# First-tile turns ahead of the second's at three projections, gated sums on VectorE, the last store in halves, compressed turns between pieces

## The reference, cut to what matters

```python
def first_block(x, p, ...):
    ...                                                            # pooled and causal attention, out projection
    x = x + rms_norm(conv_ffn(h, w_up, conv_w, conv_b, w_down), g_ffn_post)
    x = x + (p @ w_ple) * sigmoid(x @ w_ple_gate)                  # "ple" and "pg" in the kernel
    return x

def second_block(x, mem, positions, ...):
    for i in range(2):
        proj = x @ (nsa_w_in if i == 0 else mla_w_in)              # "n" and "m" in the kernel
        mix = nsa_mixer(...) if i == 0 else mla_mixer(...)         # i == 0: keys and values are also compressed
        xa = memory_cross_attention(...)
        x = layer_norm(ALPHA * x + concat(mix, xa) @ w_out[i], ...)
        x = layer_norm(ALPHA * x + hier_moe(x, ...), ...)          # 16 experts, top 2 of one group
    return x

def compress(t, pe, w1, w2):                                       # for the compressed keys and values
    blk = t[:, tok_idx] + pe                                       # 15 windows of 32 tokens
    return silu(blk @ w1) @ w2
```

## Time and profile before

| | us |
|---|---|
| median of three runs | 1104.91 (1103.94 to 1108.32) |
| the profiled execution, its own time | 1108.64 |
| its span in the profile | 1106.5 |
| TensorE busy | 1047.6 (95% of the span) |
| VectorE busy | 478.0 (43%) |
| ScalarE busy | 380.6 (34%) |
| GpSimd busy | 110.5 (10%) |

### The profile page before, as it was taken

How to read it: one execution, slowest core, us unless ns; L and a number is a source line. 1 busy time by engine, 2 the same in 40 slices (tenths; PEclk the granted TensorE clock), 3 DMA queues, 4 the chain that set the end, 5 groups by cost and what they waited for, 6 DMA issues and landing times.

```text
span 1106.5 us, 15554 instructions
## 1 busy us (share of the span) xinstructions
PE 1047.6 (95%) x6071; PEld 720.3 (65%) x6071; DVE 478.0 (43%) x1019; ACT 380.6 (34%) x739; POOL 110.5 (10%) x147
## 2 busy tenths in 40 slices
PE   6999999999999999899999999989989999999983
PEld 6967899999878879668553434338657734344431
DVE  4644656666447644765411101217664411111214
ACT  4454445555335454763211101113472311011100
POOL 0621101111000100340000000000141000000000
PEclk9999999999999999999999999999999899999997
DMA  9853576555346426317899999993427699999992
GB/s 334 194 182 117 186 226 210 170 181 201 127 178 227 138 78 232 131 53 309 339 422 422 420 421 420 419 399 131 186 108 304 249 423 421 421 420 422 418 410 85
DMA packets 95070, 296.93 MB, mean 268 GB/s; under 512 B 11102, under 2 KB 44046, under 8 KB 71438
## 3 DMA queue, kind: packets, MB, share of 16 engines
q1 hardware_dynamic: 93406, 290.09, 68.4%
q0 software_dynamic: 1584, 5.77, 1.3%
HBM read 294.60 MB, written 1.25 MB: 267 GB/s over the span
## 4 chain that ended last, share of the span: by engine, by line
PE 79%; DMA 8%; DVE 6%; ACT 3%; issue 2%; POOL 0%; POOLq 0%; SPq 0%; DVEq 0%; ACTq 0%
PE ps L902 34%; PE ps L1276 17%; PE ps L1306 8%; DMA w<-in_moe_w_up 5%; PE ps L843 3%; PE ps L1255 3%; DMA spare<-in_moe_w_down 3%; PE ps L1317 2%; PE ps L973 2%; PE ps L1006 2%; PE ps L987 2%; PE ps L896 1%; PE ps L850 1%; PE ps L1131 1%; PE ps L1209 1%
## 5 line engine op out<-in xcount | busy, mean ns | idle before, releaser
L1517 DVE TENSOR_TENSOR plo<-w,phi 128x1024 fp32r<-128x1024 f32 (+3 forms) x143 | 175.4, 1242 | 158.0 <-ACT phi L2201 157.0
L2201 ACT CAST phi<-w 128x1024 fp32r<-128x1024 f32 (+3 forms) x143 | 144.5, 1028 | 169.8 <-PE ps L902 155.6
L1276 PE MATMUL ps<-w,arena 128*64 128x512 f32 x568 | 153.5, 595 | 3.9 <-DMA w<-in_moe_w_up 3.9
L902 PE MATMUL ps<-hTr,phi 128*128 128x256 f32 x472 | 134.1, 284 | 0.0
L902 PE MATMUL ps<-hTr,plo 128*128 128x256 f32 x472 | 133.6, 283 | 0.0
L902 PE MATMUL ps<-yTr,phi 128*128 128x256 f32 x472 | 133.5, 283 | 0.0
L1276 PEld LDWEIGHTS ps<-w,arena 128*64 128x64 f32 x568 | 47.8, 137 | 78.1 <-issue 77.3
L2020 DVE CAST hots<-ps 128x256 fp32r<-128x256 f32 x16 | 6.8, 425 | 207.2 <-PE ps L1288 179.7
L902 PE MATMUL ps<-phi,yTr 128*128 128x512 f32 (+2 forms) x240 | 92.5, 385 | 3.5 <-issue 1.9
L902 PE MATMUL ps<-phi,hTr 128*128 128x512 f32 (+2 forms) x240 | 93.2, 388 | 1.1 <-DVE yTr L1507 1.1
L902 PEld LDWEIGHTS ps<-hTr,phi 128*128 128x128 f32 x472 | 90.6, 192 | 0.2 <-issue 0.2
(11 more groups left out here) (313 smaller groups left out, 1725.4 us busy)
## 6 DMA issues: line engine op xcount, KB each, us to landing
w<-in_moe_w_gate SPq DMA_DIRECT2D x36, 1024.0 KB, 15.7
w<-in_moe_w_up SPq DMA_DIRECT2D x35, 1024.0 KB, 20.2
w<-in_moe_w_down SPq DMA_DIRECT2D x29, 1024.0 KB, 21.3
w<-in_w_up SPq DMA_DIRECT2D x22, 1024.0 KB, 7.3
arena<-in_moe_w_gate SPq DMA_DIRECT2D x19, 1024.0 KB, 17.7
arena<-in_moe_w_up SPq DMA_DIRECT2D x16, 1024.0 KB, 13.9
arena<-in_moe_w_down SPq DMA_DIRECT2D x15, 1024.0 KB, 12.9
w<-in_w_out SPq DMA_DIRECT2D x6, 2048.0 KB, 9.4
```

The source lines that it names most:

```text
L902: ins_ = e.matmul(o, l[a], r[b], start=first and i == 0, stop=last and i == 2, skip_group_check=group)
L1276: ins_ = e.matmul(bank[64 * ee:64 * ee + 64, :], xg[:, k, o:o + 64], half_view(i, kind, p, ee, ab)[:, c, :], start=(k == 0), stop=(k == 7))
L1517: e.tensor_tensor(plo[:, 0:m], slots[u % 3][:, j * m:j * m + m], phi[:, 0:m].bitcast(F32), ALU.subtract).then_inc(s_cut)
L2201: e.copy(pieces[p % 4][0][:, 0:m], slots[u % 3][:, j * m:j * m + m]).then_inc(s_cast)
```

## The change

Bank plan: "x2" is parted. Tile 0 is turned into banks 4 and 5 ahead of the "ple" blocks, tile 1 into two banks of the common turn ahead of the last "ple" block. All three projections may start tile 0's half of the first piece when tile 0's low halves are there. GpSimd cuts the first piece of m0 after its join.

```diff
         B.plan("dn", 4, [4, 5, 6, 7], own=False)
+        B.plan("x2a", 2, [4, 5])
         B.work("ple", 4)
-        B.work("x2", 4)
+        B.work("x2b", 2)
...
-            for t in range(2):
-                e.wait_ge(s_x[t], 7)
-                e.dma_start(out[0, t * 128:t * 128 + 128, :], x[:, t, :]).then_inc(s_out, 16)
-            e.wait_ge(s_out, 32)
+            e.wait_ge(s_x[0], 7)
+            e.dma_start(out[0, 0:128, :], x[:, 0, :]).then_inc(s_out, 16)
+            for hf in range(2):
+                e.wait_ge(s_x[1], 7 + hf)
+                e.dma_start(out[0, 128:256, hf * 512:hf * 512 + 512], x[:, 1, hf * 512:hf * 512 + 512]).then_inc(s_out, 16)
+            e.wait_ge(s_out, 48)
...
             def tok3_steps(bks, pair, n, p0, steps, each=2, rows=None):
                 for j in steps:
                     pc = cut(p0 + j)
                     for t in range(2):
+                        if rows and j == 0:
+                            for stage, i in rows[t]:
+                                e.wait_ge(*B.empty(stage, i))
...
+            e.wait_ge(s_x[0], 2)
+            turn_row("x2a", 0, 0, x)
             e.wait_ge(*loaded("ple"))
             await_empty("p")
             for o in range(4):
                 t, hf = o // 2, o % 2
+                if o == 3:
+                    e.wait_ge(s_x[1], 2)
+                    turn_row("x2b", 0, 1, x)
                 bk = claim("ple", o)
...
-            for t in range(2):
-                e.wait_ge(s_x[t], 2)
-                turn_row("x2", 2 * t, t, x)
-            keep_on(psum[4], 9)
-            await_empty("x2")
-            out_proj("pg", h1, first_piece("pg0"))
+            out_proj("pg", h1, first_piece("pg0"), [[(stage, 0), (stage, 1)] for stage in ("x2a", "x2b")])
...
                 turn_row("x3", 2 * t, t, x)
-                keep_on(psum[4], (4, 6)[t])
-            await_empty("x3")
-            tok3("n", 0, h1, 512, first_piece("n1"))
+                if t == 0:
+                    keep_on(psum[4], 4)
+            tok3("n", 0, h1, 512, first_piece("n1"), row_tiles("x3"))
...
             bks, p0 = two_banks("n", 6), first_piece("n4")
-            tok3_steps(bks, h1, 420, p0, range(3))
+            for j in range(2):
+                for i in range(3 * j, 3 * j + 2):
+                    turn_compressed(i)
+                tok3_steps(bks, h1, 420, p0, range(j, j + 1))
+                turn_compressed(3 * j + 2)
+            e.wait_ge(s_rope, 2)
+            turn_cols("ks", pjA, 1280 - 64, 5, 64)
+            tok3_steps(bks, h1, 420, p0, range(2, 3))
...
                 turn_row("x4", 2 * t, t, x)
-                keep_on(psum[4], (2, 5)[t])
-            await_empty("x4")
-            tok3("m", 0, h1, 416, first_piece("m0"))
+                if t == 0:
+                    keep_on(psum[4], 3)
+            tok3("m", 0, h1, 416, first_piece("m0"), row_tiles("x4"))
... VectorE
-            cut(p0, p0 + 2)
-            for t in range(2):
-                turned_low("x2", 2 * t, t, (hTr, yTr))
-            cut(p0 + 2, p0 + 4)
+            turned_low("x2a", 0, 0, (hTr, yTr))
+            cut(p0, p0 + 1)
+            turned_low("x2b", 0, 1, (hTr, yTr))
+            cut(p0 + 1, p0 + 4)
...
                 ins_ = e.tensor_tensor(sgm[:, t, half], sgm[:, t, half], pl[:, t, half], ALU.mult)
-                if t == 0:
-                    ins_.then_inc(s_gm)
-                else:
-                    own.step(ins_)
-                    settle()
-                    ins_ = e.tensor_tensor(x[:, t, half], x[:, t, half], sgm[:, t, half], ALU.add)
+                own.step(ins_)
+                settle()
+                ins_ = e.tensor_tensor(x[:, t, half], x[:, t, half], sgm[:, t, half], ALU.add)
...
                 if hf:
-                    cut(p0 + 8, p0 + 10)
+                    cut(p0 + 8, p0 + 9)
                 gated(1, hf)
...
             p0 = first_piece("m0")
-            cut(p0, p0 + 1)
             for t in range(2):
                 turned_low("x4", 2 * t, t, (hTr, yTr))
+            e.wait_ge(s_cut, p0 + 1)
             cut(p0 + 1, p0 + 4)
... ScalarE
-            cast(p0, p0 + 2)
+            turned_high("x2a", 0, 0, hTr)
+            cast(p0, p0 + 1)
             for o in range(4):
+                if o == 1:
+                    cast(p0 + 1, p0 + 2)
+                if o == 3:
+                    turned_high("x2b", 0, 1, hTr)
                 evac("ple", o, pl[:, t, hf * 512:hf * 512 + 512], B.ap("ple", o)[:, :])
-            for t in range(2):
-                turned_high("x2", 2 * t, t, hTr)
... GpSimd
-            for hf in range(2):
-                half = slice(hf * 512, hf * 512 + 512)
-                e.wait_ge(s_gm, hf + 1)
-                e.drain()
-                ins_ = e.tensor_tensor(x[:, 0, half], x[:, 0, half], sgm[:, 0, half], ALU.add)
-            ins_.then_inc(s_x[0])
...
             experts(0)
+            p0 = first_piece("m0")
+            phi, plo = (a[:, 0:piece[p0][2]] for a in pieces[p0 % 4])
+            e.wait_ge(s_cast, p0 + 1)
+            e.drain()
+            e.tensor_tensor(plo, slot_of("m0")[:, 0:piece[p0][2]], phi.bitcast(F32), ALU.subtract).then_inc(s_cut)
```

More of the change, by code:

```diff
@@ L907, in cut, with tok3_steps @@
                 return [a[:, 0:piece[p][2]] for a in pieces[p % 4]]
-            def tok3_steps(bks, pair, n, p0, steps, each=2):
+            def tok3_steps(bks, pair, n, p0, steps, each=2, rows=None):
                 for j in steps:
@@ L920, in two_banks, with tok3, row_tiles @@
                 return [claim(stage, i0 + t) for t in range(2)]
-            def tok3(stage, i0, pair, n, p0):
-                tok3_steps(two_banks(stage, i0), pair, n, p0, range(4))
+            def tok3(stage, i0, pair, n, p0, rows=None):
+                tok3_steps(two_banks(stage, i0), pair, n, p0, range(4), rows=rows)
+            def row_tiles(stage):
+                return [[(stage, 2 * t + c) for c in range(2)] for t in range(2)]
             def feat3(stage, i0, pair, n, chunk, p0):
@@ L939, in pairs, with out_proj @@
                 return (2 * c + h) * 128
-            def out_proj(stage, pair, p0):
-                tok3(stage, 0, pair, 512, p0)
+            def out_proj(stage, pair, p0, rows=None):
+                tok3(stage, 0, pair, 512, p0, rows)
                 bks = [claim(stage, 2 + t) for t in range(2)]
@@ L1113, in tensor_program, with turn_compressed @@
                 e.wait_ge(*B.empty("n", i))
[L1114 to L1123, removed]
-            e.wait_ge(s_rope, 2)
-            turn_cols("ks", pjA, 1280 - 64, 5, 64)
+            def turn_compressed(i):
+                kv, c = i // 3, i % 3 * 2
+                bk = claim("kc", i)
+                m = min(2, 5 - c)
+                for q in range(2 * m):
+                    c0 = 704 + kv * 256 + (c + q // 2) * 64
+                    w = 64 if c == 4 else 128
+                    ins_ = e.transpose(bk[0:w, q * 128:q * 128 + 128], pjA[:, q % 2, c0:c0 + w], ident)
+                ins_.then_inc(B.sem_full("kc", i))
             def hidden(kv):
@@ L1568, in layer_norm @@
                 e.wait_ge(s_rstd, rooted)
-                e.scalar_tensor_tensor(x[:, t, :], z[:, t, :], rstd[:, t:t + 1], gains[1][:, :], ALU.mult,
-                                       ALU.add).then_inc(s_x[t])
+                for part in (slice(0, 512), slice(512, 1024)) if t and gain_loads == 4 else (slice(0, 1024),):
+                    e.scalar_tensor_tensor(x[:, t, part], z[:, t, part], rstd[:, t:t + 1], gains[1][:, part], ALU.mult,
+                                           ALU.add).then_inc(s_x[t])
             def rope(x1, x2, k, lo, hi_, heads, tmp, p=128):
@@ L1773, in gated @@
                 ins_ = e.tensor_tensor(sgm[:, t, half], sgm[:, t, half], pl[:, t, half], ALU.mult)
-                if t == 0:
-                    ins_.then_inc(s_gm)
-                else:
-                    own.step(ins_)
-                    settle()
-                    ins_ = e.tensor_tensor(x[:, t, half], x[:, t, half], sgm[:, t, half], ALU.add)
-                    if hf:
-                        ins_.then_inc(s_x[1])
+                own.step(ins_)
+                settle()
+                ins_ = e.tensor_tensor(x[:, t, half], x[:, t, half], sgm[:, t, half], ALU.add)
+                if hf:
+                    ins_.then_inc(s_x[t])
             for hf in range(2):
@@ L1791, in vector_program @@
                 turned_low("x3", 2 * t, t, (hTr, yTr))
-            cut(p0 + 10, p0 + 12)
+            cut(p0 + 9, p0 + 12)
             def second_row(i, c, n, last):
@@ L1961, in experts @@
                 nc.switch_bb(f"rest{i}_dve", before[i])
-                e.wait_ge(s_join, 4 * i + 4)
             iota = cst[:, C_IOTA:C_IOTA + CAP]
@@ L2160, in vector_program @@
                 e.sem_inc(s_join, 1)
+                e.wait_ge(s_join, 4 * i + 4)
                 e.br(f"rest{i}_dve")
@@ L2640, in pool_program @@
             e.memset(kcB, 0.0).then_inc(s_kcz)
+            e.drain()
```

(5 more changed lines are left out.)

1 line of the change is left out of this document (removed).

## The result

Seven executions of the changed kernel have a median of 1097.44 us (1095.12 to 1099.62), seven of the kernel before in the same comparison one of 1104.91 (1103.94 to 1113.64). The ratio is 0.9919, with a 95% interval of 0.9891 to 0.9948: faster by 0.8%, and by at least 0.52% at the near end of the interval. The prediction was 1096.7, with a range of 1093.0 to 1101.5.

A forecast was written before the change was run, and what follows sets the result against it. TensorE, busy 95% of the span, was taken as the bound, so time comes from its work or few gaps. Terms 1.9 + 2.4 + 2.7 + 0.7 + 0.5 = 8.2 us from the median 1104.91 gave 1096.7, range 1093.0 to 1101.5.

The forecast's parts named there:

- x2: Start of pg, after the down projection: pg starts behind ScalarE's copy of the last ple block, gain 1.9 us.
- x3: Start of n, after pg: earlier sums and tile 0's half first, gain 2.4 us, bounds 1.0 and 2.7.
- the turns: Compressed turns between n4's pieces: waits for ScalarE's copies hidden, gain 2.7 us, bounds 1.2 and 2.7.
- x4: Start of m, second layer: 2.4 us less 1.7 of VectorE stall, gain 0.7 us, bounds 0.0 and 2.4.
- Base: Whole kernel: gain taken from the median 1104.91, giving 1096.7; from the profiled execution's 1108.64 it would be 1100.4.
- idle stretches of about 1 us show no fall on the page: Argument against a clock fall from missed fillers, seen before x4 and between expert pieces.
- fallen fillers: Rival at x2 and x4: without fillers the clock falls to half; three falls cost 15 us, 1111.7; chance 0.05.
- the prediction's own sign: The prediction called itself wrong if the granted clock is below 1 in pg, n or m.
- End: End of the program: last step and store in halves, gain 0.5 us, bounds 0 and 0.6.
- No stall at x4: Rival at m's start: GpSimd arrives late or does not hold VectorE back, 1.7 us more, 1095.0; chance 0.12.
- The gain half given back: Rival: TensorE stands for one cast and cut at two of four places, 4.4 us lost, 1101.1; chance 0.13.
- The clock's dip moves: Rival in the experts' routing: one half-clock slice more gives 1099.2, one less 1094.2; chance 0.15.

The follow-up runs named there:

- the two kernels that undo a part: Changed kernel with tile 0's gated sums on GpSimd again: 1097.88 us; changed kernel with n waiting for both tiles' low halves: 1097.60 us.
- a kernel with 3.3 us less in its stages: Changed kernel with x2's second half in banks 6 and 7, m0's first cut on VectorE, three fillers at x3: 1096.13 us, again 1096.07.

## Why the prediction was right, and where it was not

The time, the side and the sum came out: 8.2 us were predicted from the median, the touched places gave 8.1, and the medians lie 7.5 apart. That the sum fits to a tenth is partly luck: x2, x3 and the turns came out 1.0 us above their terms together, and x4 0.9 below its own. The terms of x3, the turns and x4 lie outside the bounds that were given for them.

- **Base.** Taking the gain from the median, not from the profiled execution, was right: from 1108.64 it would have been 1100.4. The second profile of the kernel before shows the difference to be layer 2's routing.
- **x2, 1.9:** 2.04, with ScalarE's copy of the last ple block in front of pg as written; other banks took that wait away, for 0.96 us net. No kernel undid the change at x2 by itself.
- **x3, 2.4:** 2.82, above the bound of 2.7. n starts 3.6 us behind pg's end (358.28), where it was 6.6 and 3.9 was forecast; tile 1's half takes back 0.2, as forecast. As said, the fillers and not x set tile 1's turns. By the two kernels that undo a part, the row-wise start is worth 1.5 and the sums 0.7.
- **Compressed turns, 2.7:** 3.13. No claim waits and nothing is given back. The thirty transposes took 10.16 - 6.98 = 3.2 us beside the three pieces, not 3.6: row lengths overlap, and their sum was too long a price. The upper bound of 2.7 was too low for that reason.
- **x4, 0.7:** -0.24, below the bound of 0. The stall held to the tenth: VectorE's norm step took 2.98 instead of 1.28, the 1.7 that I took. Without the clock's fall the term was 1.07: with seven fillers, the second piece stands 4.0 us behind x of tile 1, where I had 4.3. The Trainium skill ("SBUF — State Buffer", SBUF: two separate sides) has the two engines exclude each other for a whole instruction; the step of 2.98 us, and 1.28 with GpSimd's cut away, agree. What failed is the step "idle stretches of about 1 us show no fall on the page": I had put fallen fillers as a rival of three falls, 15 us and a chance of 0.05. It came true at one place of three, for 1.3 us. I had written down an idle stretch of about 1.6 us ahead of tile 1's turns (1.80 measured) and then weighed it by stretches of about 1 us. By the prediction's own sign, a granted clock below 1 in m, the account of x4 was wrong.
- **End, 0.5:** 0.54 as the mean of eleven profiles with halves (18.09) against three without (18.63); single ones scatter from 17.8 to 18.7.
- **Rivals.** No stall at x4: fell. The gain half given back: fell, no place waited for a cast and cut. The clock's dip moves: in the first pair of profiles it seemed to decide by 3.4 us; the second profiles show that the routings of one program differ by 1 to 4 us between executions. That is likely why a kernel with 3.3 us less in its stages can't be told from the changed one in six or seven runs: its two profiles have 2.6 us more in layer 2's routing. The prediction also misread: the granted clock is at 8 tenths in slice 32, which is that routing, and not only low at the ends.

## What to carry to other kernels

Start a projection with the token tile that is ready, and fill waits for copies with matmuls of another unit. Undoing the first at x3 lost 1.5 us, and the second by itself gave 3.1 us; both need the next piece to be ready. Don't hand a two-input operation to GpSimd beside VectorE's chain when VectorE ends last: 1.0 us of work saved cost 1.7 of stall, and the idle time that it made on TensorE mostly went with a fall of the clock, for another 1.3. And when a microsecond is to be judged, measure the stage between two events in more than one profile; the two routings alone took 33.2 and 36.4 us in two executions of one kernel.

## What the runs showed of the hardware

- The granted clock falls to 0.50 (1.2 GHz) in stretches where TensorE counts as busy all the time: both routings, with matmuls of 16 and 20 columns and fillers. Where it falls differs between executions of one program (layer 2's routing of the kernel before: 19.47 and 15.39 us).
- 1.8 us without work ahead of m went with a fall in six of seven profiles, and the same 1.8 us ahead of n in none of one.
- Without a fall at m's start, layer 2's routing had one in five of five profiles of variants, and in one of three with the old x4; with a fall there, in none of six. Two fillers more in each routing, four of them among the router matmuls, did not keep layer 1's clock from falling (20.41 us), and seven fewer did not shorten either routing (17.33 and 18.36).
- GpSimd's subtraction of 832 columns shows 2.45 us, and VectorE's step beside it took 1.70 us longer; VectorE alone needs 1.02 for that cut. GpSimd's operation began at 747.59, within one VectorE step (746.94 to 748.22), and it was the next step that took 2.98: it got in between two steps that VectorE had back to back.
